# The end of a mixture-of-experts encoder: ten of the twelve final result tiles get help from GpSimd and ScalarE, and the last expert's down products are put in another order

## What is computed

```python
def rms_norm(x, g):
    xf = x.astype(jnp.float32)
    y = xf * lax.rsqrt(jnp.mean(xf * xf, axis=-1, keepdims=True) + EPS)
    return y.astype(x.dtype) * g
...
    gates, idx = lax.top_k(aff.T, cap)
    xe = hf[idx]
    hid = jax.nn.silu(jnp.einsum('ecd,edf->ecf', xe, w_gate)) * jnp.einsum('ecd,edf->ecf', xe, w_up)
    ye = jnp.einsum('ecf,efd->ecd', hid, w_down) * gates[..., None].astype(h.dtype)
    out = jnp.zeros_like(hf).at[idx.reshape(-1)].add(ye.reshape(-1, d))
...
        x = x + gt_f[:, None, :] * expert_choice_moe(h, w_router[l], w_gate[l], w_up[l], w_down[l])
    return rms_norm(x, g_final)
```

## Time and profile before

| what | value |
|---|---|
| median of 3 runs | 1494.31 us (1491.66 to 1494.68) |
| the profiled execution, its own time | 1494.48 us |
| its span, first to last instruction | 1492.6 us |
| PE busy | 1429.8 us (96%) |
| VectorE busy | 1034.0 us (69%) |
| ScalarE busy | 771.1 us (52%) |
| GpSimd busy | 157.3 us (11%) |
| moved by DMA | 320.89 MB, mean 215 GB/s |

### The profile page before, as it was taken

How to read it: one execution, slowest core, us unless ns; L and a number is a source line. 1 busy time by engine, 2 the same in 40 slices (tenths; PEclk the granted TensorE clock), 3 DMA queues, 4 the chain that set the end, 5 groups by cost and what they waited for, 6 DMA issues and landing times.

```text
span 1492.6 us, 22849 instructions
## 1 busy us (share of the span) xinstructions
PE 1429.8 (96%) x8655; PEld 1270.7 (85%) x8655; DVE 1034.0 (69%) x1455; ACT 771.1 (52%) x1014; POOL 157.3 (11%) x129
## 2 busy tenths in 40 slices
PE   4999999999999978999999999999999999999993
PEld 3777777888788858999999999999999999999992
DVE  3522533877778877777777777767867767767767
ACT  3422122524532344666666666666666666666564
POOL 2000000000000011022022022022022021022010
PEclk9999999999999978999999999999999999999997
DMA  9334345653521736788778778778778778778887
GB/s 340 114 105 128 128 142 169 197 200 114 155 72 36 251 130 200 246 244 248 269 242 248 270 241 249 270 242 265 254 241 268 253 240 267 255 239 252 272 264 281
DMA packets 217509, 320.89 MB, mean 215 GB/s; under 512 B 7404, under 2 KB 174392, under 8 KB 217464
## 3 DMA queue, kind: packets, MB, share of 16 engines
q1 hardware_dynamic: 208240, 293.36, 59.2%
q0 software_dynamic: 8064, 26.30, 7.6%
q10 hardware_dynamic: 1160, 0.61, 0.1%
HBM read 288.76 MB, written 31.49 MB: 215 GB/s over the span
## 4 chain that ended last, share of the span: by engine, by line
PE 87%; DVE 5%; DMA 3%; ACT 3%; issue 1%; POOL 0%; POOLq 0%; ACTq 0%; SPq 0%; DVEq 0%
PE ps L1311 27%; PE ps L1698 25%; PE ps L1696 10%; PE ps L1720 4%; PE ps L1712 4%; PE ps L1719 4%; PE ps L1711 4%; PE ps L1715 4%; PE ps L1701 1%; DVE wlo L2321 1%; DVE fin L2384 1%; PE ps L1687 1%; ACT whi L1197 1%; PE ps L1359 1%; DMA wraw<-in_w_in 1%
## 5 line engine op out<-in xcount | busy, mean ns | idle before, releaser
L1698 PE MATMUL ps<-xT,whi 128*128 128x384 f32 x2048 | 576.5, 357 | 1.6 <-DVE xT L2432 1.6
L2321 DVE TENSOR_TENSOR wlo<-raw,whi 128x2048 fp32r<-128x2048 f32 x191 | 435.4, 2293 | 193.0 <-ACT whi L1197 193.0
L1696 PE MATMUL ps<-xT,wlo 128*128 128x192 f32 x1792 | 455.4, 254 | 0.0
L1698 PEld LDWEIGHTS ps<-xT,whi 128*128 128x128 f32 x2048 | 368.3, 189 | 2.4 <-issue 1.9
L1197 ACT ACTIVATE whi<-raw 128x2048 fp32r<-128x2048 f32 x192 | 362.4, 1906 | 0.0
L1696 PEld LDWEIGHTS ps<-xT,wlo 128*128 128x128 f32 x1792 | 342.7, 191 | 0.0
L1311 PE MATMUL ps<-hT,wring 128*128 128x512 f32 x1224 | 286.7, 393 | 1.7 <-DVE hT L1834 0.9
L1311 PEld LDWEIGHTS ps<-hT,wring 128*128 128x128 f32 x1224 | 227.4, 188 | 55.0 <-issue 6.5
L1235 ACT ACTIVATE gu_l<-ps 128x384 f32<-128x384 f32 x128 | 62.9, 491 | 151.1 <-PE ps L1698 151.1
L1311 PE MATMUL ps<-wo,Yhl 128*128 128x512 f32 x576 | 135.5, 393 | 0.3 <-DVE x L2106 0.2
L1311 PEld LDWEIGHTS ps<-wo,Yhl 128*128 128x128 f32 x576 | 107.0, 188 | 22.6 <-issue 0.5
(11 more groups left out here) (245 smaller groups left out, 1543.7 us busy)
## 6 DMA issues: line engine op xcount, KB each, us to landing
raw<-in_w_gate SPq DMA_DIRECT2D x64, 1024.0 KB, 5.0
raw<-in_w_up SPq DMA_DIRECT2D x64, 1024.0 KB, 5.7
raw<-in_w_down SPq DMA_DIRECT2D x64, 1024.0 KB, 5.5
wraw<-in_w_in SPq DMA_DIRECT2D x34, 512.0 KB, 6.1
wraw<-in_w_ada SPq DMA_DIRECT2D x32, 512.0 KB, 4.9
ada_w<-in_w_ada SPq DMA_DIRECT2D x16, 512.0 KB, 12.3
acc_d<-x SPq DMA_DIRECT2D x12, 512.0 KB, 2.7
h_d<-h SPq DMA_DIRECT2D x12, 512.0 KB, 3.9
```

Of the source, the lines that this page charges most:

```text
L1696: pe.matmul(out[:, 0:CAP], wlo[:, slot, w], xT[:, k, 0:CAP], start=False, stop=False, skip_group_check=True)
L1698: mm = pe.matmul(out[:, 0:2 * CAP], whi[:, slot, w], xT[:, k, :], start=k == 0, stop=k == KB - 1, skip_group_check=True)
L2321: dve.tensor_tensor(wlo[:, j % SPL, :], raw[:, j % RAW, :], whi[:, j % SPL, :].bitcast(F32), ALU.subtract).then_inc(w_split, 1)
```

## The change

It has three parts, all at the end of the program.

1. GpSimd multiplies tiles 0, 1, 2, 3, 4, 6, 8 and 10 by `gfin_b` (`weigh`), each once it is loaded and ScalarE has its sum of squares. Two stand ahead of the gathers of `accg`, six behind them. For six of these (0, 1, 2, 3, 4, 6) VectorE only multiplies by the row factor (a `tensor_scalar` with one tensor input); for 8 and 10 ScalarE does that with an `activation`, after its copy of the sample's low part. VectorE keeps 5, 7, 9 and 11 as they were.
2. The last expert's down products: all four steps of the prompt first (`down_prompt`), then all of the sample (`down_sample`). The prompt's end has its own semaphore, `prompt_down`.
3. VectorE's order: tile groups 0 and 1, then the prompt rows (which wait for `prompt_down` alone), then groups 2 and 3, then the sample rows.

```diff
+BY_POOL = (0, 1, 2, 3, 4, 6, 8, 10)
+BY_ACT = (8, 10)
...
             for tt in range(NT):
-                sp.wait_ge(fin_ready, tt + 1)
+                n_act = len([t for t in BY_ACT if t <= tt])
+                if tt in BY_ACT:
+                    sp.wait_ge(fin_ready_act, n_act)
+                else:
+                    sp.wait_ge(fin_ready, tt + 1 - n_act)
                 sp.dma_start(out_rows(tt), fin[tt][:, :]).then_inc(fin_out, 16)
...
+            def weigh(t):
+
+                pool.wait_ge(fin_in[t], 16)
+                pool.wait_ge(ssf_ready, t + 1)
+                pool.tensor_tensor(fin[t][:, :], fin[t][:, :], gfin_b[:, :], ALU.mult).then_inc(fin_weighted, 1)
+
+            pool.wait_ge(gfin_in, 16)
+            for t in BY_POOL[0:2]:
+                weigh(t)
             pool.wait_ge(gu_filled, NE * FB)
...
+            for t in BY_POOL[2:]:
+                weigh(t)
             pool.wait_ge(fin_out, 16 * NT)
...
+            def final_scale(t):
+
+                act.wait_ge(rsf_ready, [t < end for _, end in FIN_GROUPS].index(True) + 1)
+                act.wait_ge(fin_weighted, BY_POOL.index(t) + 1)
+                act.activation(fin[t][:, :], fin[t][:, :], ACT.Copy, scale=rsf[:, t:t + 1]).then_inc(fin_ready_act, 1)
+
+            for t in BY_ACT:
+                final_scale(t)
...
+                    if last:
+                        mm = down_prompt(k)
+                        continue
...
+                if last:
+                    mm.then_inc(prompt_down, 1)
+                    for k in range(4):
+                        mm = down_sample(k)
+                    mm.then_inc(d_used, 4)
...
+                if t in BY_ACT:
+                    return
+                if t in BY_POOL:
+                    dve.wait_ge(fin_weighted, BY_POOL.index(t) + 1)
+                    dve.tensor_scalar(fin[t][:, :], fin[t][:, :], rsf[:, t:t + 1], None, ALU.mult).then_inc(fin_ready, 1)
+                    return
...
-                for n in range(len(FIN_GROUPS)):
+                for n in range(2):
...
-                dve.wait_ge(d_used, e * 4 + 4)
+                dve.wait_ge(prompt_down, 1)
...
+                for n in range(2, len(FIN_GROUPS)):
+                    final_inverse(n)
+                    for t in range(*FIN_GROUPS[n]):
+                        final_scale(t)
```

More of the change, by code:

```diff
@@ L573, in encoder_kernel @@
     ssf_ready, std_f, rsf_ready, fin_ready = sems("ssf_ready", "std_f", "rsf_ready", "fin_ready")
+    fin_weighted, prompt_down, fin_ready_act = sems("fin_weighted", "prompt_down", "fin_ready_by_act")
     accg_in, rows_sum, ssr_ready, std_r, rows_ready, rows_out, root_set = sems(
@@ L1721, in down, with down_prompt, down_sample @@
                 mm.then_inc(d_used, 1)
+            def down_prompt(k):
+                for f in (2 * k, 2 * k + 1):
+                    part = slice(0, CAP_P), slice(2 * CAP - CAP_P, 2 * CAP)
+                    start, stop = f == 0, f == FB - 1
+                    for n in range(2):
+                        w = slice(D * (f % 2) + GW * n, D * (f % 2) + GW * (n + 1))
+                        pe.matmul(ps[:, 4 + n, :], hid[:, f, part[0]], whi[:, (8 + k) % SPL, w], start=start, stop=False)
+                        pe.matmul(ps[:, 4 + n, :], hid[:, f, part[0]], wlo[:, (8 + k) % SPL, w], start=False, stop=False)
+                    for n in range(2):
+                        w = slice(D * (f % 2) + GW * n, D * (f % 2) + GW * (n + 1))
+                        mm = pe.matmul(ps[:, 4 + n, :], hid[:, f, part[1]], whi[:, (8 + k) % SPL, w], start=False, stop=stop)
+                return mm
+            def down_sample(k):
+                for f in (2 * k, 2 * k + 1):
+                    start, stop = f == 0, f == FB - 1
+                    both = hid[:, f, CAP_P:CAP_P + 2 * CAP_S]
+                    for n in range(2):
+                        w = slice(D * (f % 2) + GW * n, D * (f % 2) + GW * (n + 1))
+                        pe.matmul(ps[:, 6 + n, :], both, whi[:, (8 + k) % SPL, w], start=start, stop=False)
+                        mm = pe.matmul(ps[:, 6 + n, :], both, wlo[:, (8 + k) % SPL, w], start=False, stop=stop)
+                return mm
             def expert(e, last=False):
@@ L1740, in expert @@
                         pe.wait_ge(ye_sum, e * 1 + 1)
+                    if last:
+                        mm = down_prompt(k)
+                        continue
                     down(e, k)
-                    if k == 1 and not last:
+                    if k == 1:
                         pe.wait_ge(gu_summed, e * FB + FB)
                         tokens(e + 1)
+                if last:
[3 more added lines that the diff above has]
+                    mm.then_inc(d_used, 4)
             wait_drained(pe, "idx", 1)
```

## The result

The changed kernel takes 1503.09 us (median, 1502.18 to 1504.46) against 1494.32 us (1491.36 to 1494.88; six runs each, where the table ahead had three): a ratio of 1.0066, interval [1.0055, 1.0078]. It is slower by 8.8 us; forecast was 6.8 us slower.

What follows compares the result with a forecast made beforehand. Only the last 35 us could move, limited by VectorE's tiles (1.2 us each) and DMA writes (1.25 us). Last landing 6.8 us later: 1494.31 + 6.8 = 1501.1 us; likeliest case 1498 to 1503.5, 8-in-10 range from about 1492.5 to 1503.5.

Steps and rivals of the forecast that it cites:

- upper bound: VectorE beside GpSimd's multiplies: held between 0 and 2.3 us for each that gets in first; the upper end was taken.
- The estimate of 2.3 us for a multiply: GpSimd's multiply of one tile: half of the 4.52 us of its 128x2048 operation, 2.3 us.
- First loss: 2.3 us: Last expert's rounds: held by multiplies, VectorE ends the last hidden pieces at 1460.9 instead of 1458.6.
- rival D: GpSimd wins every turn: hidden pieces 4.9 us late, 1503.5 us; chance 0.56 together with taking turns.
- The tail: VectorE's tile work after the hidden pieces: multiplies hold it 9.2 us, and 0.9 more; last tile at 1482.8.
- The writes: End of kernel: writes of tiles 7 to 11 start at 1480.3, take 3.5 + 5.0 us, land at 1488.8.
- The slack of 1.2 us: Last expert's rows: ending on VectorE at 1483.14, while the second scatter starts only at 1484.32.
- The signs: Trace signs of taking turns: longer splits or `hid`, or idle up to 2.3 us; gathers after 1455; idle for `fin_weighted`.
- Step 3: TensorE's down products: 0.4 us to spare by the order alone, 1.9 us no longer covered once VectorE is held.
- A: Rival: multiplies cost VectorE nothing and the writes bound the end, 1493.8 us, no difference; chance 0.27.
- B: Rival: writes stop queueing, landing back at 3.5 us, 5.4 us less, 1488.9 us; chance 0.05.
- C: Rival: VectorE is never held, multiplies run only in its gaps; no change to +4 us, 1496.5 middle; chance 0.12.

Runs made afterwards that it cites:

- e4: Changed kernel with GpSimd multiplying only tiles 2, 3, 4, 6, 8 and 10, started after the last hidden pieces: 1502.20 us.
- e8: Changed kernel with GpSimd multiplying only tiles 8 and 10, behind the gathers, and ScalarE scaling these two: 1496.44 us.
- e1: Changed kernel without GpSimd's and ScalarE's work on the tiles, only the new orders kept: 1493.63 us.
- e6: Changed kernel with each of GpSimd's eight multiplies cut to 512 of 1024 columns: 1494.64 us.
- e7: Changed kernel with each of GpSimd's eight multiplies issued as two instructions of 512 columns, same work: 1500.19 us.

## Why the prediction was right in kind and too small

- **The direction and the mechanism were right.** GpSimd and VectorE take turns, and the hold lies close to the upper bound: 2.1 us for each multiply in the tail (e4, e8, and the changed kernel), of a GpSimd instruction of 2.42 us at its shortest. The estimate of 2.3 us for a multiply from half of 4.52 was 0.1 short.
- **"First loss: 2.3 us" is the term that failed.** It was 5.4. The sum let GpSimd in behind `hidf` and held only the short `hid` pieces, and it put one multiply into each round; in the trace GpSimd's waiting multiply got in right at the end of the split, ahead of `hidf` (2.54 and 2.49 us), and multiply 1 followed in the same round, ahead of `hid` (2.12). Multiply 2 held the next round's `hid` pieces (2.85), and multiply 3 the last `hidf`. Round by round VectorE falls behind by 2.4, another 1.0 and another 2.1 us, after what its waits of 1.4 us took up. This is the mechanism of rival D, which had 4.9 us and 1503.5 us for the whole; measured are 1503.09. That the sum of D comes so close is in part luck: it gave each of the first two multiplies a round of its own, and in the trace four multiplies lay in three rounds. The row with GpSimd's copy of 2.12 us had hinted at it: that copy ended 0.05 us after the split, with `hidf` already asked for.
- **The tail** was put at 10.1 us of holds (9.2 and 0.9) for five multiplies; it was 8.3 for four, since multiply 3 had already run in the rounds. So the two errors go against each other, 3.1 us too little in the rounds and 1.8 too much in the tail. With 2.6 for the prompt rows and 5.4 saved, VectorE's own account closes: 5.4 + 8.3 + 2.6 - 5.4 = 10.9, as measured, where 8.9 had been forecast.
- **The last write waits for ScalarE's tile 10** (1483.66 to 1484.82), which the sum had ready long before: ScalarE's scaling waits for the reciprocal of its group, which VectorE now makes late, and SyncE issues the writes in order. Tile 11, done at 1485.01, is written from 1485.31, 0.3 us later.
- **The writes.** Landing of the last one was put at 1488.8, 6.0 us after VectorE's last tile; it was 1490.19, 5.2 us after. The sum's rule (3.5 us for the first of five writes, 1.25 for each of the others) gives 1490.9 from their measured start at 1482.38, 0.7 us too much; its 3.5 us was no write's time in the kernel before. The saving on VectorE's own work, 5.4 us, was right, but the holds took 16.7 us. Nor could faster writes have given back more: the prompt rows, which wait for no write, came 5.4 + 8.3 - 5.4 = 8.3 us late. The slack of 1.2 us in the prediction is that of the sample rows; the prompt rows had 0.45.
- **The signs.** The longer `hid` pieces came. The gathers did not come after 1455 but at 1453.00 and 1454.32, since multiply 1 ran right behind multiply 0. And VectorE never stood idle for `fin_weighted`: it was so late itself that each multiplied tile was ready before it.
- **TensorE.** Step 3 did wait, 5.03 us and not 1.9. Behind it the granted clock was 0.50 (the 1.2 GHz level) from 1464.6 to 1470.0, and 0.99 after. It stayed off the path: the prompt's products, which ended at 1470, were used from 1478.29, and the sample's copy on ScalarE began at 1477.49, and VectorE used it at 1484.93.
- **Rivals.** A (no lasting contention) is refuted by `hidf` and tile 5; B (the writes no longer queue) was true of the queue, but as a result of the delay; C (GpSimd always loses) is refuted by the same rows.

## What to carry to other kernels

An idle GpSimd is no free help for VectorE: before moving a float32 operation with SBUF inputs onto it, ask what VectorE runs at that time, and count nearly the whole length of GpSimd's instruction as taken from VectorE's operations with two SBUF inputs and its one-input float32 scalings. Here one multiply took 2.1 us from VectorE, of 2.42, and saved it 0.5 (1.2 with ScalarE's help), so in the tail no number of tiles could pay; two already made the kernel slower. Read the length of the same instruction in both traces, since such holds appear as busy time; and where the results leave through a full write queue, some 2.5 us lost on the engines hardly change the end (0.1 us in e1, 0.6 in e6).

## What was not expected of the hardware

A GpSimd instruction that has asked during a running VectorE operation gets in at its end, ahead of VectorE's next in line (1446.61 and 1459.23 in the changed kernel). But the order of asking is not all: in e7 four half multiplies in a row kept one split out for 4.5 us, and why is not shown. GpSimd's memset of 128x512, 0.57 us each, also holds a one-input scaling on VectorE (4.09 us for four), is held by it (3.81 us for four in place of 2.28), and leaves two-input operations alone. The clock's low level, 0.50 for 5.4 us after TensorE's wait of 5.03 us, cost nothing here. TensorE's timeline of the changed kernel, with the wait in brackets:

```profile
1464.49 0.77 PE L1756 MATMUL ps<-whi,hid 128*128 128x512 f32 x1 [5.03 <-DVE hid L2394]
```

TensorE's busy time there, count of matmuls, granted clock, DMA share and GB/s in three stretches:

```profile
1459.00:1464.60 5.60, 0.57 (x4) 0.89 0.88 298
1464.60:1470.00 5.40, 5.40 (x13) 0.50 0.99 363
1470.00:1477.00 7.00, 7.00 (x31) 0.99 0.67 272
```

The middle stretch has 13 matmuls in 5.4 us, the last 31 in 7.0 us.
